# A fourth buffer for gate matrices, a new order of loads and of the first steps, in two expert layers

## The reference

```
g_sel = argmax(softmax(x @ w_group)); top_p, top_i = top_k(softmax(e_logits[g_sel]), 2)
weight = g_gate * top_p / sum(top_p)
# for each expert e, on the tokens sent to it:
h = silu(xb @ w_gate[e]) * (xb @ w_up[e]);  yb = h @ w_down[e]
out[token] += weight * yb;   h = layer_norm(ALPHA * h + out)
```

## Time and profile before

| | |
|---|---|
| median of 3 runs | 2189.38 us (2186.9 to 2190.69) |
| profiled execution, its own time | 2191.14 us |
| its span, first to last instruction | 2189.1 us |
| TensorE busy | 1851.2 us (85%) |
| VectorE, ScalarE, GpSimd busy | 36%, 17%, 7% |
| read from HBM | 562.14 MB, 257 GB/s over the span |
| expert layer 0, about | 311 to 764 us |
| expert layer 1, about | 954 to 1405 us |

### The profile page before, as it was taken

One profiled execution on the slowest core, in us unless ns is written; L12 is line 12 of the kernel. 1 busy time (PEld: TensorE's weight loads), 2 busy tenths in 40 slices (PEclk: granted clock), 3 DMA queues, 4 the chain that ended last, 5 costly groups with the idle time before them and its releaser, 6 DMA issues.

```text
span 2189.1 us, 31633 instructions
## 1 busy us (share of the span) xinstructions
PE 1851.2 (85%) x12701; PEld 1164.1 (53%) x12701; DVE 790.1 (36%) x2490; ACT 381.3 (17%) x1032; POOL 146.5 (7%) x140
## 2 busy tenths in 40 slices
PE   8999999676666699888666667698999999899998
PEld 7686555343343344455333334344588744458873
DVE  4354343221222223552221222357333524732343
ACT  2132111010111112321111011113221101322110
POOL 0112100000000020000000000000003500000250
PEclk9999999888888999899888898899999999999999
DMA  9333369999999963279999999952144237215420
GB/s 349 115 116 116 123 256 424 424 425 424 425 425 424 412 237 139 93 304 425 425 423 426 425 424 424 396 187 79 62 171 154 96 124 267 78 47 179 151 105 29
DMA packets 112375, 565.20 MB, mean 258 GB/s; under 512 B 12456, under 2 KB 15726, under 8 KB 79470
## 3 DMA queue, kind: packets, MB, share of 16 engines
q1 hardware_dynamic: 112238, 563.21, 64.6%
HBM read 562.14 MB, written 1.05 MB: 257 GB/s over the span
## 4 chain that ended last, share of the span: by engine, by line
PE 65%; DMA 22%; issue 6%; DVE 4%; ACT 3%; SPq 1%; DVEq 0%; ACTq 0%
PE ps L2498 14%; DMA ring<-in_moe_w_gate_dram 12%; PE ps L1666 11%; DMA arena<-in_moe_w_gate_dram 9%; PE ps L689 8%; PE ps L2528 6%; PE ps L1232 5%; PE ps L296 3%; PE ps L1338 3%; PE ps L1242 3%; PE ps L729 2%; PE ps L2013 1%; ACT arena L1803 1%; PE ps L1695 1%; PE ps L1764 1%
## 5 line engine op out<-in xcount | busy, mean ns | idle before, releaser
L689 PE MATMUL ps<-ring,arena 128*32 128x256 f32 x2816 | 217.6, 476 | 157.0 <-issue 129.5
L2498 PE MATMUL ps<-arena,ring 128*128 128x256 f32 (+1 forms) x1536 | 305.5, 362 | 0.0
L2498 PEld LDWEIGHTS ps<-arena,ring 128*128 128x128 f32 x1536 | 271.9, 190 | 33.9 <-issue 1.0
L1666 PE MATMUL ps<-ring,arena 128*128 128x512 f32 (+1 forms) x576 | 252.5, 598 | 4.5 <-DVE arena L421 4.5
L689 PEld LDWEIGHTS ps<-ring,arena 128*32 128x32 f32 x2816 | 123.3, 136 | 245.9 <-issue 221.5
L705 DVE TENSOR_TENSOR arena<-arena,ps 64x256 f32<-64x256 f32 x64 | 27.2, 425 | 499.7 <-ACT arena L699 499.6
L1666 PEld LDWEIGHTS ps<-ring,arena 128*128 128x128 f32 x576 | 110.4, 194 | 137.8 <-issue 137.5
L689 PE MATMUL ps<-arena 128*32 128x256 f32 x1280 | 100.4, 482 | 69.7 <-issue 69.7
L2627 DVE SCALAR_TENSOR_TENSOR arena<-ps,pcol,arena 128x255 f32<-128x255 f32 (+1 forms) x176 | 84.9, 482 | 181.3 <-ACT arena L2566 178.2
L2597 POOL TENSOR_TENSOR arena<-arena 128x256 f32<-128x256 f32 x44 | 55.3, 1257 | 1248.6 <-DVE arena L2627 1248.6
L1232 PE MATMUL ps<-arena,ring 128*128 128x256 f32 x512 | 115.3, 384 | 1.8 <-DMA ring<-in_ssm_w_in_dram 1.6
(11 more groups left out here) (330 smaller groups left out, 2166.3 us busy)
## 6 DMA issues: line engine op xcount, KB each, us to landing
ring<-in_moe_w_gate_dram SPq DMA_DIRECT2D x44, 2048.0 KB, 33.8
ring<-in_moe_w_up_dram SPq DMA_DIRECT2D x44, 2048.0 KB, 38.4
ring<-in_moe_w_down_dram SPq DMA_DIRECT2D x44, 2048.0 KB, 38.8
ring<-in_w_up_dram SPq DMA_DIRECT2D x22, 2048.0 KB, 7.9
arena<-in_moe_w_gate_dram SPq DMA_DIRECT2D x20, 2048.0 KB, 33.5
arena<-in_moe_w_up_dram SPq DMA_DIRECT2D x20, 2048.0 KB, 38.0
arena<-in_moe_w_down_dram SPq DMA_DIRECT2D x20, 2048.0 KB, 38.0
ring<-in_ssm_w_in_dram SPq DMA_DIRECT2D x12, 2048.0 KB, 9.5
```

Source lines behind the costliest of these rows:

```text
L689: mm = nc.tensor.matmul(ps[j * CAP:(j + 1) * CAP, 5, 0:256], xg[:, b, (k % 2 * 4 + k // 2) * CAP:(k % 2 * 4 + k // 2 + 1) * CAP], w[:, k, ...
L1666: mm = nc.tensor.matmul(ps[:, bank + n % 4, 0:n_cols], xT[:, k, tt * P:(tt + 1) * P], w[:, k, :], start=(k == 0), stop=(k == KD - 1))
L2498: mm = nc.tensor.matmul(ps[:, n % 4, lo:hi], w[:, k, k4 * P:(k4 + 1) * P], xT_mlp[:, k, lo:hi], start=(k == 0), stop=(k == KD - 1))
```

## The change

Loads and buffers:

- Gate matrices get four buffers (`GATES = 4`), expert e uses buffer e % 4: ring slot 0, ring slot 3, the new one (2), and the third set's old one (3). The new one is not one piece: k-tiles 0 to 3 lie at arena column 22160 (1 MB, 8 KB in a partition), 4 and 5 in `h[:, 0, :]`, 6 and 7 at arena 5376 (0.5 MB each, 4 KB in a partition). Each of its loads is three DMAs.
- Up and down keep three buffers. Gate e waits for gate and up of expert e-4, and SP's order is up(e), gate(e+1), down(e).
- `sp_third(sp, 0)` loads gate 3 in place of gate 2; `sp_extra`, after `sp_third(sp, 2)`, loads gate 2 into the new buffer. Its middle piece waits for the norm of the first 128 tokens.
- At the end the next stage's first chunk is issued right behind down(31); the norm's rows come after gate and up of expert 30 are read, behind `sp_next`. `alpha_id` moves from arena 22160 to `pcol`.

Order at the head: ScalarE does step_pick_copy of expert 0 before `act_exps`; VectorE does `dve_weights` after step_xg of expert 0 and step_slots of expert 1, just before the tally.

The seventh step_combine (experts 24 to 27) comes before the gate and up of expert 28 (before the branch on `crowded`).

```diff
-        alpha_id = area(22160, P)
+        alpha_id = pcol[:, 0:P]
+        EXTRA = ((0, 4, area(22160, 4, FF)), (4, 6, h[:, 0, :].rearrange("p (k n) -> p k n", k=2)),
+                 (6, 8, area(5376, 2, FF)))
...
+            def sp_extra(sp):
+                sp_gate(sp, 2, 2, extra_loaded.sem, (0, 2))
+                sp.wait_ge(half_act.sem, half_act.at(1))
+                sp.wait_ge(half_dve.sem, half_dve.at(1))
+                sp_gate(sp, 2, 2, extra_loaded.sem, (1,))
...
             def experts_sp(sp):
-                def load(e, slot):
-                    for part in range(3):
-                        used = m["down"] if part == 2 else m["gateup"]
-                        sp.wait_ge(used.sem, used.at(e - 2))
-                        sp_load(sp, e, slot, part, slot_loaded(slot, part))
+                def load_gate(e, buf):
+                    sp.wait_ge(m["gateup"].sem, m["gateup"].at(e - 3))
+                    sp_gate(sp, e, buf, gate_loaded(buf))
...
+                def load(e, n):
+                    load_up(e, n % 3)
+                    load_gate(e + 1, (n + 1) % GATES)
+                    load_down(e, n % 3)
...
-                sp.wait_ge(residual_in.sem, residual_in.at(1))
-                sp_rows(sp, t["ln_ffn_g"][layer], t["ln_ffn_b"][layer])
+                ring.issue(sp, ring.issued + 1)
                 for used in (m["gateup"], m["down"]):
                     sp.wait_ge(used.sem, used.at(NE - 2))
                 if sp_next:
                     sp_next(sp, 0)
+                sp.wait_ge(m["gateup"].sem, m["gateup"].at(NE - 1))
+                sp_rows(sp, t["ln_ffn_g"][layer], t["ln_ffn_b"][layer])
...
+                step_combine(pe, m, m["rows_act"].at(NE - 4), m["back_copied"].at(QUADS - 1), 4, m["combined"])
                 pe.wait_ge(crowd.sem, crowd.at(1))
...
             def experts_act(act):
+                step_pick_copy(act, m, lambda s: s.at(1), None, 0)
                 head.act_exps(act)
-                step_pick_copy(act, m, lambda s: s.at(1), None, 0)
...
                     if first_quad(q) and i == 0:
+                        head.dve_weights(dve)
                         head.dve_tally(dve)
...
                 step_slots(dve, m, lambda s: s.at(1), None, 0, 0)
-                head.dve_weights(dve)
                 step_xg(dve, m, lambda s: s.at(1), None, 0)
...
             experts0.sp_third(sp, 2)
+            experts0.sp_extra(sp)
             experts0.sp(sp)
```

More of the change, by code:

```diff
@@ L136, in issue, with skip @@
         self.issued = max(self.issued, min(upto, len(self.chunks)))
+    def skip(self, c, loads):
+        self.skipped.append((c, loads))
     def arrived(self, pe, c, turn=0):
-        pe.wait_ge(self.loaded[c % RING_SLOTS], 16 * (c // RING_SLOTS + 1 + turn))
+        fewer = sum(loads for after, loads in self.skipped if c > after and c % RING_SLOTS == after % RING_SLOTS)
+        pe.wait_ge(self.loaded[c % RING_SLOTS], 16 * (c // RING_SLOTS + 1 - fewer + turn))
 def cols8(w, a, b):
@@ L810, in make_experts @@
                 c = first + 3 * (e - NE // 3)
[L811 removed]
+                ring.release(c, m["gateup"], e - 1)
                 ring.release(c + 1, m["gateup"], e + 1)
                 ring.release(c + 2, m["down"], e + 1)
[L814 to L816 removed]
+            for buf in range(2):
+                ring.skip(first + 3 * (NE - NE // 3) - 6 + 3 * buf, 11 - QUADS)
@@ L830, in sp_third, with sp_gate @@
-            def sp_third(sp, part):
-                sp_load(sp, 2, 2, part, third_loaded[part].sem)
-            def experts_sp(sp):
-                def load(e, slot):
-                    for part in range(3):
-                        used = m["down"] if part == 2 else m["gateup"]
-                        sp.wait_ge(used.sem, used.at(e - 2))
-                        sp_load(sp, e, slot, part, slot_loaded(slot, part))
-                with sp.Fori(1, NE // 3) as third:
-                    for slot in range(3):
-                        load(3 * third + slot, slot)
+            def sp_gate(sp, e, buf, signal, pieces=range(3)):
+                src = t["moe_w_gate"][layer, bass.ds(e, 1)].rearrange("e (p k) n -> p (e k) n", p=P)
+                if buf == 2:
+                    for lo, hi, dst in (EXTRA[i] for i in pieces):
+                        sp.dma_start(dst, src[:, lo:hi, :]).then_inc(signal, 16)
+                else:
+                    sp.dma_start(third_gate if buf == 3 else ring.rows8(first + 3 * buf), src).then_inc(signal, 16)
@@ L877, in arrived @@
                             ring.arrived(pe, first + 3 * slot + part, use)
-                    for part in range(2):
-                        arrived(part)
-                    step_gateup(pe, m, v, b, w[0], w[1])
+                    if i == 2:
+                        pe.wait_ge(extra_loaded.sem, extra_loaded.at(48 * (q + 1)))
+                    elif i == 3:
+                        pe.wait_ge(third_loaded[0].sem, third_loaded[0].at(16 * (q + 1)))
+                    else:
+                        ring.arrived(pe, first + 3 * i, q)
+                    arrived(1)
+                    step_gateup(pe, m, v, b, gates[i], ups[slot])
                     if not is_last(q, i):
```

80 lines of the change are left out of this document (56 added, 24 removed).

## The result

| | before | changed |
|---|---|---|
| median | 2189.55 us (2186.9 to 2190.69, 4 runs) | 2173.22 us (2171.74 to 2174.5, 4 runs) |
| span of the profiled execution | 2189.1 us | 2170.7 us |
| ratio | | 0.9928, 95% interval 0.9916 to 0.9941 |

The kernel is 16.3 us faster, 11.2 were forecast (range 2173.0 to 2186.0, which holds the median by 0.2 us). On another chip the changed kernel took 2173.27 us (2172.11 to 2174.22, 5 runs), ratio 0.9924 (0.9911 to 0.9938). So direction and mechanism held, and about a third of the gain was not in the sum.

The account below looks back on a forecast made before the run. The stream of expert matrices after the queue's restart was taken as the bound. 9.82 - 1.45 + 2.84 = 11.2 us off the profiled 2191.14 gave 2179.9, or 2178.2 from the median; range 2173 to 2186.

Parts of the forecast that it names:

- The bound: Both expert layers: the DMA stream of matrices sets their length, counted from the queue's restart after the first gate and up.
- The fourth buffer: Expert layers: one matrix fewer after the restart, 4.91 us a layer, less 1.5 us in both layers for smaller packets.
- The load order: Order up(e), gate(e+1), down(e): no issue waits longer, TensorE's split idle time may move the clock, not the stream; 0 us.
- The head: Pick to first gate and up: earlier copy and later weights start the products 1.42 us earlier, 2.8 us in both layers.
- rival (a): Layer 0's first gate and up: less idle time keeps the clock from falling, 2.8 us more, 2175.4; chance 0.2.
- The end: After expert 31: early chunk wins nothing, rows and parameters still arrive in time; cost 0, a few us if margin is used.
- The seventh combine: Moved ahead of expert 28: delays its gate and up by a few us, which later experts' slack makes up; cost 0.
- (b): New buffer's packets cost the 2 KB price and the head gives nothing: 2188.3, or half of each, near 2182.5; chance 0.1.
- (c): New gate's extra DMAs each pay a fixed cost in the stream: 3.3 us each, 92 us in all, 2272; chance 0.04.
- (d): Another buffer's release gates the issues, so the stream is not shortened and only the head is left: 2186.5; chance 0.06.
- the pair of zeros on TensorE's clock: 0 us forecast for the first gate and up's duration and for expert 31's gate and up to its down product.

Follow-up runs that it names:

- experiment 1: The kernel before with only the new head order (ScalarE's pick copy before the exponentials, VectorE's weights later): 2182.24 us, ratio 0.9971.
- experiment 6: The changed kernel with 16 more matrices a layer (fourth-place gates, third-set ups) cut in three DMAs: 2179.35 us, ratio 0.9959.
- experiment 5: The changed kernel with load order up(e), down(e), gate(e+1): 2177.16 us, ratio 0.9943.
- experiment 2: The changed kernel with the old order at the head: 2183.09 us, ratio 0.9970.
- experiment 3: The changed kernel with the old head order, TensorE's idle stretch there filled with products nobody reads: 2178.52 us, ratio 0.9948.
- experiment 7: Two separate edits of the changed kernel: next stage's first chunk not issued early, 2170.69 us; seventh combine back inside expert 28's step, 2172.86 us.
- before_awake: The kernel before with filler products: 2 before and 8 after the head's first turn, 14 behind expert 30's down product; 2209.45 us, ratio 1.0094.

## Why the prediction was right, and where its size was off

The bound. Right: the layers are as long as the stream behind the restart, and experiments 1 and 6 moved the restart and the stream apart from each other.

The fourth buffer, forecast 4.91 a layer less packets. Right: 85 matrices in place of 86, the extra one in the hole. The packets' price was taken as 0.10 us a matrix from loads that did not fill the queue, and with nothing for the half in 8 KB packets; in the full stream it is 0.15 to 0.17. 14 of them cost 2.4 us and not 1.45. The bounds (0 to 8.7) held it.

The load order, "no issue waits longer", cost and gain 0. The timing was right and the price wrong by two terms. The order covers the restart, as the kernel before did with gate 3 and up 3: with the down load second on SP the layer is 2 us longer (experiment 5), a trap that the count of matrices does not show. And it moves TensorE's idle time. The forecast said that this "may move the granted clock, not the stream", and left it without a price; it was worth 0.8 and 2.9 us from expert 31's gate and up to the down product, which is on the path because behind expert 31 no load of a later expert hides it. With the same order seven ends of 18 were slow, so the size of this term is partly luck.

The head, forecast 1.42 a layer. The gap was right to 0.01 us, but a gap on TensorE has a second price. That was rival (a), with chance 0.2. It came, and experiments 1 to 3 show that it was not an even chance: with a gap of 3.56 us the products were slow in three heads of four, with 2.14 in one of 18. "In layer 1 as much idle time let the clock stand" was one case, read as a coin; the other traces say that it was the lucky one. The Trainium skill (TensorE: Matmul & The Clock Gate, "What's actually happening") says that the gate's window runs free of the kernel. By that the two profiles of the changed kernel could be expected to differ. They don't at the marks above, and do at the next stage's first products in layer 1 (9.32 and 7.75 us); two profiles are too few to say more.

The end, cost 0. The rows and the parameters came in time: TensorE's turn of the parameters in layer 1 begins at 1388.01, 3.51 us behind the combine's start at 1384.50, as before (1404.91 and 1401.40). Not seen was that down 31 would become the last to arrive once gate and up are fast: 1.28 us of wait in layer 0.

The seventh combine, cost 0: right (experiment 7). Rivals (b), (c) and (d) fell: the stream is 3.7 us shorter in each layer, so another buffer's release does not gate it, and a cut matrix costs 0.15 to 0.17 us, neither the 2 KB price of 0.62 nor 0.40 for each of two more DMAs.

So the step that was mis-sized is the pair of zeros on TensorE's clock. Measured, they are 2.8 + 0.8 + 2.9 = 6.5 us in the traces, against 1.0 that the cut matrices took back. The forecast's other terms, 11.2 us, came out as 10.2. The time lies at the very end of the range because the first and the last gate and up ran at 2.4 GHz in both layers; rival (a), 2175.4, had only the first of layer 0 in it.

## What to carry to other kernels

In a kernel bound by a stream of loads the few products that stand between two streams are on the path, and TensorE comes to them from an idle stretch: price them at both levels of the clock, and count a shortened gap twice, once for itself and once for the clock that may come back. An idle stretch of known length can be filled with products that nobody reads; measure one call of the filler in the trace first, for the fillers that were three to four times too long cost 20 and 14 us where the right ones won 7. Compare two kernels between the same marks of their traces, since stages that nobody touched moved by more than 3 us here. Count not only the matrices ahead of the last product but also what may be issued at the restart: one load must cover the wait of the next.

## What the runs showed of the hardware

- A 128x512 float32 product of `pe_stay_awake` is recorded as two and takes 0.88 us at 2.4 GHz (8 calls in a row 7.03 us in before_awake, with the granted clock at 1.00).
- A matrix cut in 8 KB and 4 KB pieces costs 0.15 to 0.17 us more in the full queue than one in 16 KB pieces, half as much again as the forecast had worked out from loads that did not fill the queue; three DMAs in place of one cost no more than that.
- The behaviour of the clock mostly repeated: two profiles of the same kernel gave first and last gate and ups of 3.66 to 3.67 us in all four places and 9.60 and 9.59 us for the next stage's first products of layer 0. What still differed were these products in layer 1, 9.32 and 7.75 us.
